# The last LayerNorm of a decoder layer: scale weight multiplied into the rows early, offset and bias as TensorE products

## The reference

```
def layer_norm(x, g, b):
    mu = jnp.mean(x32, axis=-1, keepdims=True)
    var = jnp.mean(jnp.square(x32 - mu), axis=-1, keepdims=True)
    return (x32 - mu) * lax.rsqrt(var + LN_EPS) * g + b
...
h = layer_norm(alpha * h + 0.5 * swiglu(h, ffn2_w_gate[l], ffn2_w_up[l], ffn2_w_down[l]), ln3_g[l], ln3_b[l])
return h[:, N_META:]
```

## Time and profile before

| what | us |
|---|---|
| median of 3 runs | 1124.66 (1124.59 to 1128.49) |
| profiled execution | 1125.31 |
| its span | 1123.6 |
| TensorE's last large product ends | 1105.06 |
| VectorE's last piece ends | 1121.15 |

### The profile page before, as it was taken

How to read it: one execution, slowest core, us unless ns; L and a number is a source line. 1 busy time by engine, 2 the same in 40 slices (tenths; PEclk the granted TensorE clock), 3 DMA queues, 4 the chain that set the end, 5 groups by cost and what they waited for, 6 DMA issues and landing times.

```text
span 1123.6 us, 15984 instructions
## 1 busy us (share of the span) xinstructions
PE 1077.6 (96%) x6569; PEld 932.0 (83%) x6569; DVE 475.1 (42%) x739; ACT 342.8 (31%) x437; POOL 144.0 (13%) x100
## 2 busy tenths in 40 slices
PE   8999999999999999999997999999999999999993
PEld 7999999999999987688865568768888888888882
DVE  4332323323232353699985533453333333322235
ACT  3322223222212144433227532352222232211211
POOL 5000000000111124252312003240000000000001
PEclk9999999999999999999998999999999999999997
DMA  6433242331333223122210101223333333142311
GB/s 191 113 80 106 75 110 76 85 90 55 101 89 92 89 75 97 38 80 72 76 38 1 38 1 40 74 75 82 105 86 101 92 95 99 53 139 86 95 51 75
DMA packets 159165, 90.34 MB, mean 80 GB/s; under 512 B 6596, under 2 KB 156792, under 8 KB 159128
## 3 DMA queue, kind: packets, MB, share of 16 engines
q1 hardware_dynamic: 159128, 89.83, 28.2%
HBM read 87.72 MB, written 2.10 MB: 80 GB/s over the span
## 4 chain that ended last, share of the span: by engine, by line
PE 81%; DVE 12%; ACT 3%; POOL 2%; issue 1%; DMA 0%; DVEq 0%; SPq 0%; POOLq 0%
PE ps L913 72%; POOL xl L484 2%; PE ps L1322 2%; DVE sc L1587 2%; DVE top L1586 2%; PE ps L1048 1%; PE ps L1302 1%; PE ps L1313 1%; DVE x L1539 1%; DVE zrow L1497 1%; DVE qk L1624 1%; PE ps L1330 1%; DVE sil L1533 1%; PE ps L1110 1%; ACT whi L617 1%
## 5 line engine op out<-in xcount | busy, mean ns | idle before, releaser
L913 PE MATMUL ps<-xh,whi 128*128 128x264 f32 (+1 forms) x1264 | 356.5, 331 | 3.8 <-DVE wlo L1406 1.6
L913 PE MATMUL ps<-xl,whi 128*128 128x264 f32 (+1 forms) x1264 | 351.1, 330 | 7.7 <-POOL xl L484 6.8
L913 PE MATMUL ps<-xh,wlo 128*128 128x264 f32 (+1 forms) x1264 | 353.2, 330 | 0.0
L913 PEld LDWEIGHTS ps<-xl,whi 128*128 128x128 f32 x1264 | 212.5, 190 | 34.8 <-POOL xl L484 14.6
L913 PEld LDWEIGHTS ps<-xh,whi 128*128 128x128 f32 x1264 | 213.2, 190 | 30.7 <-issue 5.4
L913 PEld LDWEIGHTS ps<-xh,wlo 128*128 128x128 f32 x1264 | 213.9, 189 | 21.5 <-issue 0.2
L1397 DVE TENSOR_TENSOR wlo<-wraw,whi 128x2048 fp32r<-128x2048 f32 (+1 forms) x79 | 166.9, 2113 | 143.5 <-ACT whi L617 143.5
L617 ACT ACTIVATE whi<-wraw 128x2048 fp32r<-128x2048 f32 (+1 forms) x89 | 152.4, 1712 | 129.6 <-PE ps L913 124.0
L913 PE MATMUL ps<-hh,whi 128*128 128x264 f32 (+1 forms) x528 | 141.7, 322 | 0.0
L913 PE MATMUL ps<-hl,whi 128*128 128x264 f32 (+1 forms) x528 | 141.3, 322 | 0.0
L913 PE MATMUL ps<-hh,wlo 128*128 128x264 f32 (+1 forms) x528 | 140.5, 320 | 0.0
(11 more groups left out here) (217 smaller groups left out, 881.2 us busy)
## 6 DMA issues: line engine op xcount, KB each, us to landing
wraw<-in_ffn_w_gate SPq DMA_DIRECT2D x44, 512.0 KB, 4.0
wraw<-in_ffn_w_up SPq DMA_DIRECT2D x43, 512.0 KB, 5.2
wraw<-in_ffn_w_down SPq DMA_DIRECT2D x32, 384.0 KB, 3.4
wraw<-in_ffn_w_down SPq DMA_DIRECT2D x32, 320.0 KB, 3.9
wraw<-in_w_in SPq DMA_DIRECT2D x19, 512.0 KB, 4.7
wraw<-in_w_out SPq DMA_DIRECT2D x8, 512.0 KB, 4.0
xin<-in_x SPq DMA_DIRECT2D x2, 1024.0 KB, 5.9
out<-zrow SPq DMA_DIRECT2D x8, 256.0 KB, 2.0
```

What stands on the lines that cost most here:

```text
L913: mm = pe.matmul(ps[:, b + e, 0:width], w, mov, start=(first and n == 0), stop=(last and n == 2))
```

## The change

`gain` takes the place of the first half of `gb`, broadcast to 128 partitions; the second half goes, and `gain_bias` is a tile of two partitions with g in the first and b in the second, loaded by two small DMAs. Behind the statistics of each block VectorE multiplies the block of `zrow` by g, in place (`scale_rows`); that of block 7 is issued behind the variance. Then the output is rstd * (z * g) + (-mean * rstd) * g + b. The last two terms are a product of two rows: the four columns of -mean * rstd, each beside a column of ones, are transposed by TensorE to two rows (bank 6), ScalarE copies them to SBUF, and TensorE makes one product for each half row, in all eight PSUM banks. VectorE finishes each half row with one instruction that reads PSUM. ScalarE's and GpSimd's pieces are gone.

```diff
             zrow = sb("zrow", [P, 4, D], F32, s)
-            gb = sb("gb", [P, 2, D], F32, s)
+            gain = sb("gain", [P, D], F32, s)
+            gain_bias = sb("gain_bias", [2, D], F32, s)
...
+        offset = sil[:, 0, 208:216].rearrange("p (j n) -> p j n", j=4)
+        offset_rows = sil[0:2, 1, 0:SEQ]
...
-                    sp.dma_start(gb[:, 0, :], a["ln3_g"].broadcast_to([P, D])).then_inc(gb_in, 16)
-                    sp.dma_start(gb[:, 1, :], a["ln3_b"].broadcast_to([P, D])).then_inc(gb_in, 16)
+                    sp.dma_start(gain[:, :], a["ln3_g"].broadcast_to([P, D])).then_inc(gb_in, 16)
+                    sp.dma_start(gain_bias[0:1, :], a["ln3_g"]).then_inc(gb_in, 16)
+                    sp.dma_start(gain_bias[1:2, :], a["ln3_b"]).then_inc(gb_in, 16)
...
-            for i, q in enumerate(POOL_HALVES):
-                pool.wait_ge(scaled, i + 1)
...
-                pool.tensor_tensor(half_row(zrow, q), half_row(zrow, q), gb[:, 1, 512:1024], ALU.add).then_inc(out_pool, 1)
...
-            for i, q in enumerate(POOL_HALVES):
-                act.wait_ge(centred, q + 1)
-                act.activation(half_row(zrow, q), half_row(zrow, q), ACT.Copy, scale=rstd3[:, q // 2:q // 2 + 1])\
-                    .then_inc(scaled, 1)
+            act.wait_ge(offset_turned, 1)
+            act.activation(offset_rows, ps[0:2, 6, :], ACT.Copy).then_inc(offset_copied, 1)
...
+            def affine_rows():
+
+                pe.wait_ge(gb_in, 16 * 3)
+                pe.wait_ge(z_copied, KT)
+                pe.wait_ge(offset_ready, 1)
+                for j in range(4):
+                    mm = pe.transpose(ps[0:2, 6, j * P:(j + 1) * P], offset[:, j, :], ident[:, :])
+                mm.then_inc(offset_turned, 1)
+                pe.wait_ge(offset_copied, 1)
+                for q in range(8):
+                    pe.matmul(ps[:, (q + 7) % 8, :], offset_rows[:, (q // 2) * P:(q // 2 + 1) * P],
+                              gain_bias[:, (q % 2) * 512:(q % 2 + 1) * 512], start=True, stop=True).then_inc(affine_ready, 1)
...
+                if not (isinstance(m, int) and m == KT - 1):
+                    scale_rows(m)
+
+            def scale_rows(m):
+
+                dve.wait_ge(gb_in, 16 * 3)
+                dve.wait_ge(bst3_done, 4 * m + 4)
+                v = zrow[:, :, bass.ts(m, P)]
+                dve.tensor_tensor(v, v, gain[:, bass.ts(m, P)].unsqueeze(1).broadcast_to([P, 4, P]), ALU.mult)\
+                    .then_inc(rows_scaled, 1)
...
-                centre(0)
+                scale_rows(KT - 1)
+                dve.memset(offset[:, :, 1], 1.0)
                 dve.wait_ge(sd3_done, 1)
                 link(dve.reciprocal(rstd3, sd3))
-                for q in range(1, 8):
-                    centre(q)
-                    if q - 1 not in POOL_HALVES:
-                        finish(q - 1)
-                finish(7)
+                dve.scalar_tensor_tensor(offset[:, :, 0], mv3[:, :, 0], -1.0, rstd3, ALU.mult, ALU.mult).then_inc(offset_ready, 1)
+                dve.wait_ge(rows_scaled, KT)
+                for q in range(8):
+                    dve.wait_ge(affine_ready, q + 1)
+                    v = half_row(zrow, q)
+                    dve.scalar_tensor_tensor(v, v, rstd3[:, q // 2:q // 2 + 1], ps[:, (q + 7) % 8, :], ALU.mult, ALU.add)\
+                        .then_inc(out_done, 1)
```

More of the change, by code:

```diff
@@ L314, in build @@
         sd3_done = sem("sd3_done")
[L315 to L318, removed]
+        offset_ready = sem("offset_ready")
+        offset_turned = sem("offset_turned")
+        offset_copied = sem("offset_copied")
+        affine_ready = sem("affine_ready")
+        out_done = sem("out_done")
+        rows_scaled = sem("rows_scaled")
         stored = sem("stored")
-        POOL_HALVES = (1, 3, 5)
         def half_row(v, q):
@@ L457, in _ @@
             for q in range(8):
[L458 to L461, removed]
+                sp.wait_ge(out_done, q + 1)
                 sp.dma_start(out[0, (q // 2) * P:(q // 2 + 1) * P, (q % 2) * 512:(q % 2 + 1) * 512], half_row(zrow, q))\
@@ L595, in _ @@
             norm_lo(1)
-            for i, q in enumerate(POOL_HALVES):
-                pool.wait_ge(scaled, i + 1)
-                if i == 0:
-                    pool.wait_ge(gb_in, 32)
-                pool.tensor_tensor(half_row(zrow, q), half_row(zrow, q), gb[:, 1, 512:1024], ALU.add).then_inc(out_pool, 1)
         @block.scalar
@@ L1382, in _ @@
             ffn(2)
+            affine_rows()
         @block.vector
```

## The result

The changed kernel is slower: 1134.0 us median (1129.96 to 1135.5, 9 runs) against 1127.03 (1124.18 to 1129.69, 9 runs); the ratio is 1.0057, 95% interval 1.0043 to 1.0071, or 6.4 us (the medians lie 7.0 apart). The forecast was 1.05 us faster, and the range ended at 1126.0. The prediction had only the first three runs of the kernel before, with a median of 1124.66, and the nine together have 1127.03. Against either the measured time lies above the range: its upper end is 1.3 us over the kernel before, and 6.4 was measured.

What follows compares the result with a forecast made beforehand. TensorE was taken to bound the kernel outside the tail, and VectorE's run of pieces the tail. The last piece would end at 1120.10 instead of 1121.15, so 1124.66 - 1.05 = 1123.6 us; range 1121.4 to 1126.0.

Steps and rivals of the forecast that it cites:

- Ahead of the tail: Before the last residual: seven added multiplications of 0.69 us and the wait for gain rows cost nothing.
- Steps 1 to 4: Tail, last multiplication, offsets, four transposes (1.1 us) and ScalarE's copy: offsets ready at 1110.42, copy done at 1112.17.
- Step 5: Tail, eight two-row fp32 products on TensorE: 0.85 us apart, first result at 1113.41, eighth at 1119.38.
- third rival: Tail products take four passes, 1.7 us each: 6.8 us later, 1130.4 us in all; chance 0.03.
- Step 6: Tail, VectorE's eight finishing pieces wait for the products, 0.69 us each; last ends at 1120.10, 1.05 earlier.
- Step 7: Tail, stores follow 0.85 us apart and keep pace; the 2.4 us behind the last piece stay.
- The clock: Tail, TensorE's granted clock is 0.50 (1.2 GHz) while the products run.

Runs made afterwards that it cites:

- paired kernel: The changed kernel with a second copy of the rows at partitions 64 and 65, used by odd half rows; 1127.12 us, ratio 0.9998 to the kernel before.

## Why the prediction was wrong

**Ahead of the tail: right.** The seven multiplications took 0.69 us each, VectorE did not wait for the gain row, the statistics span 96.9 us against 96.8, and TensorE is busy without a gap in 94.9 us of the down projections of both kernels.

**Steps 1 to 4: right in sum.** The offsets were ready 5.1 us after the last residual's start where 5.3 was worked out (the memset took 0.06 us and ran beside the reciprocal), the transposes took 1.01 at the low clock (1.1), the copy 0.59. TensorE started the products 6.97 us after the residual; 7.09 was forecast.

**Step 5 failed**: "So I take 0.85 between products that all lie on the same rows of the array." It was 1.71. At that step the rows were read wrongly in two ways that fit together. In the earlier trace rows L1147 has x4 while its code makes two products. The prediction took 0.43 us for a product at full clock and doubled it for the low one; but 0.43 was the time of an instruction, and a product has two. And L1279 was taken to show one product after another, each of two instructions over both halves of the array; it shows two products at a time on different rows, and its eight heads give sixteen instructions:

```profile
L1279 PE MATMUL ps<-qa,wuk x16: 589/1057/1219, 590.4 to 596.1; 64*128 64x512 f32 x16
```

The trace of the kernel before had the right price. At 720.70 `keep_warm` makes 32 plain fp32 products (`WARM_NORM`), and the row has 64 instructions. Ahead of it L1033 makes two products, one call each, with 512 columns and all 128 rows; they start 0.86 us apart at a granted clock of 1.00, and twice that, for 0.50, is 1.72:

```profile
718.98 1.02 PE L1033 MATMUL ps<-x,mean_w 128*128 128x512 f32 x2
719.84 1.02 PE L1033 MATMUL ps<-sil,mean_w 128*128 128x512 f32 x2
720.70 7.31 PE L1018 MATMUL ps<-mean_w 128*128 128x128 f32 x64
```

The paired kernel shows that this reading is the right one: of the experiments, only there does plain fp32 cost 0.85 a product at 1.2 GHz. The price of the error is 7 x 0.853 = 6.0 us between first and last product and 0.8 on the first (it was ready 9.1 us after the residual's start; 8.3 was forecast). Together that is the 6.8 us of the third rival, and the forecast of 1.05 less turns into 5.7 more in the tail.

That rival had a chance of 0.03. The Trainium skill (FP8 and Floating Point Precision, TensorE Precision Notes) gives true fp32 four passes; the trace agrees: 1.71 us is 4 x 512 columns at 1.2 GHz, and the reduced form took a quarter, 0.427. The objection that the prediction raised against it came from the misread rows. Of the other rule of the Trainium skill (TensorE: Matmul & The Clock Gate, Part 3: Packing small matmuls), which lets a weight load overlap a running product only on another row group, the trace shows the opposite, and the measurement decides: each instruction of L1379 has a weight load of 0.33 onto the same rows, beside the instruction before it, and the spacing is 0.853 all the same. That the loads are hidden was forecast rightly, though the row of L1147 was read with the wrong count.

**Step 6** was right in kind (VectorE waits for each product), with 0.75 us for a piece where 0.69 was taken. **Step 7** was right too: the stores kept pace, and the end lies 2.4 us behind the last piece (1130.0 to 1132.4).

**The clock** was forecast rightly: 0.50 under all products. That it has to do with the few rows is borne out by one trace of each kind: with two rows it fell from 0.98 to 0.50 and stayed at 0.50, with 128 it came back to 1.00.

**What was worth something.** Fewer VectorE pieces and no GpSimd promised 5.6 us. VectorE waits 4.0 us for the first product and, with pieces 1.71 apart where they could be 0.67, 7 x 1.04 = 7.3 for the others: 5.6 - 4.0 - 7.3 = -5.7. With products in the reduced form the same plan makes the tail 2.6 us shorter than before, and without the round of transposes 4.2. But 1.0 us of each is to be had without any product, by taking the GpSimd pieces away, so what the plan itself gives is 1.6 and 3.2. What the lost low bits do to the result was not measured.

## What to carry to other kernels

Before a row's duration is taken as the price of an operation, divide its xcount by the number of calls in the code that made them, and look whether neighbours used other rows of the array. A stage that TensorE enters after a pause is priced at the low clock; here, with products of two rows, it stayed there for all 14 us. Where the precision allows it, an affine term of a few rows belongs into the reduced fp32 form, with high and low parts as further rows: four rows left the same tail as two (15.95 and 15.9). Helping VectorE by GpSimd pieces on the same tiles can cost more than it saves: each of the three pieces here held VectorE up by 1.0 us and saved it 0.66.

## What was not expected of the hardware

- Dense products of two rows let the granted clock fall: 0.98 in 1116.35 to 1119.9, 0.50 from 1120.1 to 1127, with TensorE busy without a gap in both stretches. The same products with 126 rows of zeros added brought it from 0.51 (1115.0 to 1120.9) to 1.00 (1121.1 to 1125.0). Each is one trace.
- Two products of two rows, at partitions 0 and 64, take the time of one: 7.20 us for sixteen instructions against 14.02, at a clock of 0.50 in both.
- Weight loads onto the same rows did not lengthen a product: loads of 0.33 us, and instructions 0.853 apart, with TensorE busy for 14.01 of 14.20 us.
- A VectorE piece beside a GpSimd addition took 1.75 us instead of 0.75; with no GpSimd work none did.
